# The last products of a run by seven in another order, their follow-up ahead of the last fold, and a weight split moved up

## What is computed

```python
def conv_ffn(x, w_up, conv_w, conv_b, w_down):
    h = x @ w_up
    L = h.shape[1]
    hp = jnp.pad(h, ((0, 0), (CONV_W - 1, 0), (0, 0)))
    hc = conv_b
    for j in range(CONV_W):
        hc = hc + hp[:, j:j + L] * conv_w[j]
    u, g = jnp.split(hc, 2, axis=-1)
    return (jax.nn.silu(g) * u) @ w_down
...
        h = h + (jax.nn.silu(f @ w_gate[i]) * (f @ w_up[i])) @ w_down[i]
```

## Time and profile before

| | us |
|---|---|
| median of 3 runs (2271.45 to 2273.67) | 2271.45 |
| the profiled execution's own time | 2273.23 |
| span of the profiled execution | 2272.0 |
| TensorE busy (99% of the span) | 2245.7 |
| VectorE busy (62%) | 1399.7 |
| ScalarE busy (45%) | 1028.0 |

### The profile page before, as it was taken

How to read it: one execution, slowest core, us unless ns; L and a number is a source line. 1 busy time by engine, 2 the same in 40 slices (tenths; PEclk the granted TensorE clock), 3 DMA queues, 4 the chain that set the end, 5 groups by cost and what they waited for, 6 DMA issues and landing times.

```text
span 2272.0 us, 38521 instructions
## 1 busy us (share of the span) xinstructions
PE 2245.7 (99%) x15555; PEld 2017.7 (89%) x15555; DVE 1399.7 (62%) x2549; ACT 1028.0 (45%) x1890; POOL 98.3 (4%) x171
## 2 busy tenths in 40 slices
PE   9999999999999999999999999999999999999998
PEld 7798999999997898999899788978899888888997
DVE  5356576759743465667588566869454465455663
ACT  5256554447533465543376443223244444223652
POOL 3001100000000001000000000100000000000001
PEclk9999999999999999999999999999999999999999
DMA  6545776245434436632365272743222222223651
GB/s 212 157 129 150 187 186 180 98 143 173 135 95 124 116 113 161 196 106 96 115 173 161 81 203 76 189 111 102 93 66 65 66 93 93 93 96 119 185 167 51
DMA packets 90132, 292.78 MB, mean 129 GB/s; under 512 B 12721, under 2 KB 16723, under 8 KB 89187
## 3 DMA queue, kind: packets, MB, share of 16 engines
q1 hardware_dynamic: 79587, 215.69, 29.6%
q0 software_dynamic: 9792, 73.57, 14.0%
q10 hardware_dynamic: 576, 1.05, 0.1%
HBM read 288.14 MB, written 71.34 MB: 158 GB/s over the span
## 4 chain that ended last, share of the span: by engine, by line
PE 88%; DVE 7%; ACT 3%; issue 2%; DMA 0%; POOL 0%; SPq 0%; DVEq 0%; ACTq 0%; POOLq 0%
PE G L1349 61%; PE G L1386 8%; PE G L1459 7%; DVE wL L2334 2%; PE X L1386 1%; PE X L1671 1%; PE X L1626 1%; PE X L1753 1%; PE X L1649 1%; ACT wH L1799 1%; DVE Av L2696 1%; DVE Av L2699 1%; PE X L1737 1%; PE X L1454 1%; PE X L1722 1%
## 5 line engine op out<-in xcount | busy, mean ns | idle before, releaser
L1799 ACT ACTIVATE wH<-raw 128x512 fp32r<-128x512 f32 (+3 forms) x648 | 459.0, 726 | 503.1 <-PE G L1349 429.9
L2334 DVE TENSOR_TENSOR wL<-raw,wH 128x512 fp32r<-128x512 f32 (+3 forms) x648 | 521.3, 815 | 224.8 <-ACT wH L1799 222.0
L1349 PE MATMUL G<-aH,wH 128*128 128x264 f32 (+2 forms) x2112 | 548.2, 321 | 4.4 <-DVE wL L2334 4.1
L1349 PE MATMUL G<-aL,wH 128*128 128x264 f32 (+2 forms) x2112 | 526.5, 311 | 0.0
L1349 PE MATMUL G<-aH,wL 128*128 128x264 f32 (+2 forms) x2112 | 526.2, 311 | 0.0
L1349 PEld LDWEIGHTS G<-aH,wH 128*128 128x128 f32 x2112 | 346.1, 189 | 35.6 <-issue 10.1
L1349 PEld LDWEIGHTS G<-aH,wL 128*128 128x128 f32 x2112 | 344.0, 188 | 22.0
L1349 PEld LDWEIGHTS G<-aL,wH 128*128 128x128 f32 x2112 | 344.6, 188 | 19.1 <-issue 0.2
L2493 DVE TENSOR_TENSOR hT<-G,hT 128x528 f32<-128x528 f32 (+1 forms) x83 | 58.0, 699 | 166.8 <-PE G L1349 166.7
L1386 PE MATMUL G<-seven,wH 128*128 128x264 f32 (+2 forms) x792 | 146.7, 284 | 1.3 <-DVE wL L2334 1.2
L1349 PE MATMUL G<-hidH,wH 128*128 128x264 f32 (+1 forms) x528 | 140.8, 321 | 3.3 <-DVE wL L2334 2.6
(11 more groups left out here) (401 smaller groups left out, 3788.3 us busy)
## 6 DMA issues: line engine op xcount, KB each, us to landing
raw<-weights SPq DMA_DIRECT2D x210, 512.0 KB, 3.7
weight_sums<-weights POOLq DMA_DIRECT2D x72, 704.0 KB, 6.7
raw<-weights SPq DMA_DIRECT2D x48, 704.0 KB, 4.1
raw<-weight_sums SPq DMA_DIRECT2D x132, 256.0 KB, 3.0
raw<-weights SPq DMA_DIRECT2D x99, 256.0 KB, 2.9
weight_sums<-weight_sums POOLq DMA_DIRECT2D x24, 704.0 KB, 4.8
raw<-weights SPq DMA_DIRECT2D x12, 384.0 KB, 6.0
negc<-sums POOLq DMA_DIRECT2D x16, 264.0 KB, 5.7
```

The lines of the kernel that those rows point to most:

```text
L1349: done = e.matmul(m.pair(i)[0:M, bank, 0:n], a[:, k, 0:M], b[:, kx, lo - t0:lo - t0 + n], start=(k == 0 and c == 0), stop=(k == nk - 1 and ...
L1799: e.activation(m.high(i)[:, c], m.raw(i)[:, c], ACT.Copy).then_inc(s.w_hi, 1)
L2334: e.tensor_tensor(m.low(i)[:, c], m.raw(i)[:, c], m.high(i)[:, c].bitcast(F32), ALU.subtract).then_inc(s.w_lo, 1)
```

## The change

In the last part of a run by seven (pairs jj = 9 and 10, called 9 and X below) the products come in another order. Before: 9/6, X/1, 9/7, X/2, X/5, 9/3, X/6, 9/4, X/7, X/3, X/4. Now: 9/6, X/1, 9/7, X/5, X/6, 9/3, X/7, 9/4, X/2, X/3, X/4. All pieces that are still open are issued ahead of the last fold, and the split of down 1 stands between `silu7` and `gate7` of pair X. All three runs are changed.

```diff
@@ by_seven
         else:
-            out += [(jj, 6), (nx, 1), (jj, 7), (nx, 2), (nx, 5), (jj, 3), (nx, 6), (jj, 4), (nx, 7), (nx, 3), (nx, 4)]
+            out += [(jj, 6), (nx, 1), (jj, 7), (nx, 5), (nx, 6), (jj, 3), (nx, 7), (jj, 4), (nx, 2), (nx, 3), (nx, 4)]
     return out
@@ seven, in schedule
             step("prod7", f, half, jj, p)
+            if ROLE[i + 1][0] != "seven":
+
+
+                while pieces:
+                    step(*pieces.popleft())
             step({1: "p1st", 2: "c11", 5: "p5th", 6: "u2nd", 7: "c22", 3: "c12", 4: "c21"}[p], f, half, jj)
...
             yield
-        while pieces:
+        for n in range(len(pieces)):
             step(*pieces.popleft())
+            if len(pieces) == 3:
+                for what in splits_at(state["next"]):
+                    step(*what)
         yield
```

## The result

| | before | changed |
|---|---|---|
| median of 13 runs, us | 2272.85 (2271.45 to 2274.57) | 2278.43 (2275.61 to 2279.73) |
| ratio to before, 95% interval | 1 | 1.0022 (1.0014 to 1.0029) |
| span of the profiled execution, us | 2272.0 | 2277.5 |
| TensorE busy, us | 2245.7 | 2249.8 |
| mean granted clock of a run, lowest to highest | 0.998 to 0.999 (33 runs beside the first experiments) | 0.995 to 0.997 (all 13 runs) |

The change makes the kernel 5.6 us slower by the medians, about 0.2%. The forecast was 2271.2 us in a range of 2269.3 to 2274.8. Of the 7.2 us between forecast and median, 1.4 us are the base alone: the kernel before has a median of 2272.85 us in 13 runs, where the forecast started from 2271.45 us in three. The first rival had the mechanism and a chance of 0.16.

What follows compares the result with a forecast made beforehand. TensorE, busy for nearly all of 2272.0 us, was taken as the bound. Gains of 0.07 us (f = 0) and 0.13 us (f = 1) make -0.2 us; from the median 2271.45, forecast 2271.2 us, range 2269.3 to 2274.8.

Steps and rivals of the forecast that it cites:

- The first rival: Ends of f = 0 and f = 1: the joined wait halves TensorE's clock, losing 3.4 us, giving 2274.7 us; chance 0.16.
- The pot: TensorE's four waits at the ends of f = 0 and f = 1: 4.96 us, 6.0 us in all with restarts.
- what moves into the place of the waits: Down 0's k = 10, f = 0 and f = 1: one new wait for `hidl7`, 2.9 us, replaces both old ones.
- Part 1: New order of products: TensorE's wait for `c22` before X/4 goes; down 0 starts 1.46 us earlier with the restart.
- I put `gate7` at 596.4, 0.1 later: Pair 9's gate on VectorE, f = 0: starts at 596.4 instead of 596.29, as `c11` of X moves into this stretch.
- Part 2: Pieces ahead of the last fold: pair 9's `hidh7` on ScalarE no longer waits for `c21` and starts 0.56 us earlier.
- Part 3: Down 1's split between X's `silu7` and gate, f = 0: gives back 0.46 us of a 0.53 us gain.
- Sum of the schedule: Whole kernel: 0.07 us gained in f = 0 and 0.13 in f = 1, together -0.2 us.
- f = 2: Third run by seven: no wait to remove and none added; `hidl7` is hidden with 1.0 us to spare.
- The clock: TensorE behind the joined wait, f = 0 and f = 1: granted clock stays 1.00 after 2.9 us idle, costing nothing.
- The price of the fall: Behind each joined wait: 4.00 us at a mean clock of 0.57 lose 1.7 us, 3.4 us for two places.
- the edge of 0.2%: Whole kernel: 0.2%, 4.5 us, can be told from no change; slower by more than that was given 0.04.

Runs made afterwards that it cites:

- the first experiments: First of three groups of follow-up runs, each on one chip beside 33 runs of the kernel before; those medians are 2273.08, 2273.09 and 2272.98 us.
- the wait filled: Changed kernel plus 20 unread matmuls of 128x264 ahead of down 0's last step, f = 0 and 1: 2274.18 us, ratio 1.0006.
- three steps: On the changed kernel, cumulatively: down 1's split in halves, 2270.21 us; third piece of down 0's split later, 2269.55; pair 8's hidden low part first, 2268.69.
- Filling the first wait: Kernel with new order and pieces ahead, without the split between, plus 8 unread matmuls ahead of down 0's k = 10: 2273.15 us, ratio 1.0002.

## Why the prediction was wrong

Point by point:

- **The pot, and what moves into the place of the waits: right.** Both waits went, and one wait for `hidl7` came, in f = 0 and f = 1 alone. It is 3.09 and 3.18 us long; 2.9 was forecast, and 2.7 to 3.1 named as the sign, so the second is just outside.
- **Part 1, the wait for `c22`: right.** Down 0 starts 1.42 and 1.37 us earlier (1.46 forecast).
- **"I put `gate7` at 596.4, 0.1 later": wrong, mis-sized by 0.5 us.** It came 0.63 us later than before. I had let `c11` of X out of its old place on VectorE and moved up all behind it. But the low part behind it needs the high copy of X/2's weights, and ScalarE makes that behind `hidh7` of pair 8 and `p5th` of X. In the new order VectorE therefore stands idle for 0.57 us (the row at 588.62), and a fold more, `c11`, follows later. Putting pair 8's hidden low part into this idle time gave 0.44 and 0.46 us back, which shows that it was on the chain.
- **Part 2, 0.56 us for the pieces ahead of the fold: right in size, wrong in whose it is.** In the old order it measured 0.63 and 0.65 us alone. In the new order it is worth nothing, since X/4 and `c21` are early enough by the new order alone. The prediction has X/4's end at 595.9, before pair 9's gate at 596.4, but doesn't draw this from it. It counts the 0.56 us once, so its sum is not touched.
- **Part 3, 0.46 us given back: right**; alone it measured 0.47 and 0.42.
- **Sum of the schedule**: -0.2 us forecast, +0.64 measured with the wait filled (at down 2). The failing term is the 0.5 us of `gate7` above, twice. This alone would have left the time within 0.2%.
- **f = 2: right.** No wait came. `hidl7` of X ends at 2211.66 + 0.69 = 2212.35, 5.86 us behind the start of down 0 at 2206.49 (read from the chain that ended last, as 2200.98 was); 5.9 was forecast.
- **The clock: this is the step that failed.** I took the likeliest to be that it holds behind 2.9 us, which puts nothing for it into the sum, and gave its fall a chance of 0.16, though the text says itself that this wait is nearer to the 3.9 us behind which it fell than to the 1.3 behind which it held. Measured is a granted clock of 0.50 behind the wait of 3.09 us, and half clock behind that of 3.18 us. With the rows at hand the fall deserved a far higher chance. What brought the chance down was one comparison, "1 us shorter than the only one behind which it fell", which is no evidence that it holds.
- **The price of the fall**: 1.7 us was taken for each place, from the start of the program. Measured were 2.75 and 1.5 us. The range ended at the rival's sum of 2274.8, with no room for a slow stretch that lasts longer than the one seen. With 2.75 + 1.5 for the clock and 0.64 for the schedule the sum is 4.9 us, and the span grew by 5.5, of which 0.6 lies elsewhere, as said above.

The measured result lies just beyond the edge of 0.2% that the text had drawn for slower, to which it gave 0.04.

## What to carry to other kernels

When an edit joins two waits of TensorE, price the joined wait as a new thing: summed idle time is not what counts, since the half clock behind one wait of 3.1 us cost here up to 2.75 us more. Where a chain on VectorE and ScalarE sets the end, changing the order of what TensorE does, or of two things in series on the chain, only moves the wait; what helps is to cut independent work small enough to fit the idle gaps between dependent steps. Here this moved down 1 in three steps from 0.4 us later than before (wait filled) to 2.4 us earlier. And a queue position that an instruction leaves free is worth nothing until the instruction behind it has its input: follow the releaser of each one before moving it up.

## What the runs showed of the hardware that was not expected

- **Idle time counts with what is near it.** At the ends of the runs by seven, waits of 1.2 to 1.3 us, 1.0 us of matmuls apart, brought the clock down in two of four places in the profiles of two kernels, and in the other two it held. Behind single waits up to 1.9 us, behind waits of 1.4 and 1.5 us with some 7.5 us of work between them, and behind 0.5 and 2.4 to 2.5 us with some 7 us between them, it held there wherever a profile was taken. The Trainium skill, "TensorE: Matmul & The Clock Gate", Part 1, under "A second HAM failure mode: psum-queue depth-cycling", tells of small idle gaps between groups of matmuls that bring the clock down repeatedly; the rows of the two kernels agree with it: gaps of a length that left the clock alone when single did bring it down together.
- **The length of a wait alone doesn't decide.** One might take a bound from the waits above; the start of the program warns against it. TensorE waits there in every kernel for its first weights, behind 32 matmuls of 128x128. In the profile of the kernel with down 1's split in halves this wait is 2.15 us and the mean granted clock from 11 to 15 us is 0.60; in that of the kernel with the pieces ahead alone it is 3.51 us and the clock stays at 1.00. TensorE's timelines and the busy times of the two:

```profile
10.32 0.48 PE L1358 MATMUL G<-aH,wH 128*128 128x264 f32 x2 [2.15 <-DVE wL L2343]
11.00:15.00 4.00, 4.00 (x23) 4.00 (x23) 4.00 (x7) 4.00 (x8) 3.63 (x4) 0.60 1.03 401
```
```profile
10.77 0.48 PE L1354 MATMUL G<-aH,wH 128*128 128x264 f32 x2 [3.51 <-DVE wL L2339]
11.00:15.00 4.00, 3.85 (x31) 3.67 (x31) 4.00 (x7) 4.00 (x8) 3.63 (x5) 1.00 1.04 402
```

  This is also the place from which the prediction took its one wait with a fall and its price. In the other 13 profiles the clock is down there, behind waits of 2.15 to 4.15 us.
- **The same program can take either course.** The kernel with new order and pieces ahead ran between 2271.7 and 2278.1 us, against 2271.7 to 2275.0 for the one before in the same group. Filling the first wait closed most of this. A spread that widens under a change is thus itself a sign to look at the granted clock.
- **The length of the slow stretch varies**: some 6 us for f = 0 and some 3.5 us for f = 1 behind waits of nearly the same length, at a price of 2.75 and 1.5 us. The two falls behind pairs of short waits cost 2.7 us each. What sets the length isn't shown by these runs.
